# Moving the PSUM evacuation of the attention heads' outputs from VectorE to ScalarE

## The reference

```python
def windowed_gqa_attention(h, w_qkv, w_o, sink):      # h: 1024 tokens x 1024, already normed
    q, k, v = split(h @ w_qkv)                        # 16 query heads, 4 key/value heads, 64 wide
    def block(qi, i):                                 # 128 queries against up to 384 keys
        logits = einsum('bqkgd,bskd->bkgqs', qi, kb) - slopes * dist   # masked outside the window
        m = maximum(max(logits), sink)
        p = exp(logits - m)
        probs = p / (sum(p) + exp(sink - m))
        return einsum('bkgqs,bskd->bqkgd', probs, vb)
    return concat(blocks) @ w_o
```

## Time and profile before

| | |
|---|---|
| median of 3 runs | 2630.5 us |
| profiled execution | 2631.06 us, of which the span is 2629.4 us |
| busy in the span | PE 2330.4 us (89%), DVE 1869.7 us (71%), ACT 1552.1 us (59%), POOL 282.9 us (11%) |
| mean granted TensorE clock | 0.951 |
| first attention | from the start to about 469 us |
| L575, ScalarE's copies of the turned tiles | 88 |
| L657, VectorE's copies of the heads' outputs | 64 |

### The profile page before, as it was taken

How to read it: one execution, slowest core, us unless ns; L and a number is a source line. 1 busy time by engine, 2 the same in 40 slices (tenths; PEclk the granted TensorE clock), 3 DMA queues, 4 the chain that set the end, 5 groups by cost and what they waited for, 6 DMA issues and landing times. The chain is left out here.

```text
span 2629.4 us, 34467 instructions
## 1 busy us (share of the span) xinstructions
PE 2330.4 (89%) x11464; PEld 1758.9 (67%) x11464; DVE 1869.7 (71%) x2461; ACT 1552.1 (59%) x2036; POOL 282.9 (11%) x260
## 2 busy tenths in 40 slices
PE   7899989569999999929999999998955999999991
PEld 6666658447777777727777777776844777777671
DVE  5775572668898888858556666556256888888895
ACT  5554460447777777735555565555043778777772
POOL 0000020012121111030000000002001122211102
PEclk9999999779999999959999999999977999999996
DMA  3012020469999999852000000002146999999995
GB/s 121 25 55 96 24 72 32 170 227 397 392 395 399 402 394 395 338 174 89 24 24 24 24 24 24 0 24 72 32 171 206 390 394 401 398 394 393 403 360 212
DMA packets 129501, 538.48 MB, mean 205 GB/s; under 512 B 23232, under 2 KB 52032, under 8 KB 80288
## 3 DMA queue, kind: packets, MB, share of 16 engines
q1 hardware_dynamic: 110496, 470.62, 47.1%
q0 software_dynamic: 18944, 67.12, 7.3%
HBM read 487.50 MB, written 50.20 MB: 204 GB/s over the span
## 5 line engine op out<-in xcount | busy, mean ns | idle before, releaser
L1507 DVE TENSOR_TENSOR m_lo_gate<-m_raw_gate,m_hi_gate 128x2048 fp32r<-128x2048 f32 x132 | 298.9, 2290 | 81.7 <-ACT m_hi_gate L1502 79.8
L1507 DVE TENSOR_TENSOR m_lo_up<-m_raw_up,m_hi_up 128x2048 fp32r<-128x2048 f32 x128 | 292.5, 2285 | 7.1 <-ACT m_hi_up L1502 7.0
L1507 DVE TENSOR_TENSOR m_lo_down<-m_raw_down,m_hi_down 128x2048 fp32r<-128x2048 f32 x124 | 280.2, 2283 | 13.7 <-ACT m_hi_down L1502 13.7
L1502 ACT CAST m_hi_down<-m_raw_down 128x2048 fp32r<-128x2048 f32 x124 | 236.2, 1907 | 90.7 <-DMA m_raw_down<-in_moe_w_down_dram 54.8
L1502 ACT CAST m_hi_gate<-m_raw_gate 128x2048 fp32r<-128x2048 f32 x132 | 247.8, 1908 | 25.6 <-DMA m_raw_gate<-in_moe_w_gate_dram 25.4
L1502 ACT CAST m_hi_up<-m_raw_up 128x2048 fp32r<-128x2048 f32 x128 | 244.4, 1911 | 22.2 <-DMA m_raw_up<-in_moe_w_up_dram 21.2
L1622 PE MATMUL m_G<-m_hi_gate,m_x_hi 128*96 128x512 f32 x512 | 206.1, 402 | 11.4 <-DVE m_x_lo L1732 11.3
L1622 PE MATMUL m_U<-m_hi_up,m_x_hi 128*96 128x512 f32 x512 | 205.2, 401 | 0.0
L1623 PE MATMUL m_G<-m_hi_gate,m_x_lo 128*96 128x512 f32 x512 | 204.6, 400 | 0.0
L1624 PE MATMUL m_G<-m_lo_gate,m_x_hi 128*96 128x512 f32 x512 | 202.5, 395 | 0.0
L1623 PE MATMUL m_U<-m_hi_up,m_x_lo 128*96 128x512 f32 x512 | 201.8, 394 | 0.0
(11 more groups left out here) (380 smaller groups left out, 4907.9 us busy)
## 6 DMA issues: line engine op xcount, KB each, us to landing
m_raw_gate<-in_moe_w_gate_dram SPq DMA_DIRECT2D x128, 1024.0 KB, 11.1
m_raw_up<-in_moe_w_up_dram SPq DMA_DIRECT2D x128, 1024.0 KB, 12.8
m_raw_down<-in_moe_w_down_dram SPq DMA_DIRECT2D x124, 1024.0 KB, 12.0
out_rows<-m_y POOLq DMA_DIRECT2D x64, 384.0 KB, 7.5
a1n_rows<-in_diff_w_qkv_dram SPq DMA_DIRECT2D x21, 512.0 KB, 5.5
out_rows<-a0n_gain SPq DMA_DIRECT2D x1, 8064.0 KB, 37.3
x_res<-in_x_dram SPq DMA_DIRECT2D x4, 1024.0 KB, 9.6
a0n_rows<-in_swa_w_o_dram SPq DMA_DIRECT2D x8, 512.0 KB, 3.3
```

Source lines behind the costliest of these rows:

```text
L1502: act.copy(self.hi[w][:, cut], self.raw[w][:, cut]).then_inc(self.hi_done[w], 1)
L1507: eng.tensor_tensor(self.lo[w][:, cut], self.raw[w][:, cut], self.hi[w][:, cut].bitcast(F32), ALU.subtract)\
```

## The change

`heads_out` goes from VectorE's program to ScalarE's. The two `tensor_copy` become two `act.copy` of the same operands. On ScalarE they stand behind the copies of block `i` and concern block `i-1`; those of block 7 stand behind the loop. On VectorE the calls are taken out, and nothing is put in their place. Semaphores and counts stay as they are.

```diff
@@ scalar engine, group(g, last_group)
+                    def heads_out(i):
+                        act.wait_ge(pv_done, 8 * g + i + 1)
+                        out = O[:, i % 2, :].rearrange("p (h n) -> p h n", h=QH)
+                        for e, part in enumerate(HALVES):
+                            last = act.copy(oT[part, i, bass.ds(2 * g, 2), :], out[part, e:QH:2, :])
+                        last.then_inc(oT_ready, 1)
@@
                             act.copy(pT[:, i % 2, j, :], TB[:, (before[i] + j) % 2, :]).then_inc(pT_ready, 1)
+                        if i >= 1:
+                            heads_out(i - 1)
                         if i == 3 and not last_group:
                             projections.high_part(act, g + 1, 2)
+                    heads_out(NT - 1)
@@ vector engine, group(g, last_group)
-                    def heads_out(i):
-                        dve.wait_ge(pv_done, 8 * g + i + 1)
-                        out = O[:, i % 2, :].rearrange("p (h n) -> p h n", h=QH)
-                        for e, part in enumerate((slice(0, 64), slice(64, 128))):
-                            last = dve.tensor_copy(oT[part, i, bass.ds(2 * g, 2), :], out[part, e:QH:2, :])
-                        last.then_inc(oT_ready, 1)
@@
                             normalise(i)
-                        if i >= 1:
-                            heads_out(i - 1)
                         if i == 4 and not last_group:
                             projections.low_part(dve, g + 1, 2)
                     if last_group:
                         o_part(0)
                         o_part(1)
-                    heads_out(NT - 1)
```

## The result

The changed kernel takes 2648.7 us in the median of 4 runs (2645.9 to 2650.7) against 2630.3 before: ratio 1.0066, 95% interval 1.0050 to 1.0082, 18.4 us slower. I had predicted 15.3 us slower, 2645.8 us, with a range of 2638 to 2652. The profiled execution took 2648.4 us (span 2646.7).

The account below looks back on a forecast made before the run. TensorE sets the loops' pace, with ScalarE very near and VectorE third. Losses of 9.4 us in three groups, 3.3 in the last and 2.6 at its end sum to 15.3 us slower: 2645.8 us, range 2638 to 2652.

Parts of the forecast that it names:

- Rival D: VectorE as hidden pacemaker: freeing 0.86 us in each of 32 blocks shortens them; 4.4 us faster, 2626.1; chance 2%.
- h = 0.87 us: ScalarE's cost per heads_out: 0.11 us of lost overlap plus two copies of 0.38 us.
- The offset `2 * g`: Dynamic offset on ScalarE, computed while the third copy runs, at nothing; some 0.1 us if not covered.
- 3.14 us a group: Loss in each of groups 0 to 2, summed over the block steps; 9.4 us in three.
- 3.33 in the last group: Last group's steps: 0.87 for block 1 to 2, 2.44 for four steps, 0.02 for block 6 to 7.
- no wait for `a_snk`: Sign in the last group: ScalarE's 0.26 us wait for VectorE's stats disappears, hiding part of the new copies.
- 2.57 at the end: Behind the last group, L587 queues behind heads_out(7), so the output projection starts 2.57 us later.
- rival B: The gap at the last group's end drops TensorE's clock, costing 1.4 to 2 us more; 2647.5 us; chance 25%.
- the prediction's own sign: Listed as proving the prediction wrong: a clock below 1 behind 378 us, which would point to rival B.
- the bare forecast: The forecast alone, h near 0.87 and TensorE's clock kept: 15.3 us slower, 2645.8 us; chance 45%.
- Rival A: The 64-partition copies on ScalarE overlap, so h = 0.55; sum 8.8 us slower, 2639.3 us; chance 15%.
- C: ScalarE's copies cost more than their columns say, near h = 1.29; sum 24.6 us slower, 2655.1 us; chance 10%.

Follow-up runs that it names:

- the gap placement: Changed kernel with heads_out(i-1) on ScalarE moved between its second and third copy of block i; ratio 1.0011, 2.9 us slower than before by the ratio.
- without copies: Changed kernel without the 64 copies, ScalarE only waiting and signalling, so later work computes on other data; ratio 1.0074.
- the parts: Two kernels with heads_out on ScalarE only in groups 0 to 2 (ratio 1.0036), or only in the last group (1.0030), on VectorE otherwise.
- the kernel with matmuls in the gap: Changed kernel with three extra 512-column matmuls on TensorE, useless for the output, behind the last product; ratio 1.0055.
- the last group alone: heads_out on VectorE in groups 0 to 2 and on ScalarE in the last group; ratio 1.0030, 7.3 us slower than before at the medians.
- the full-height kernel: Changed kernel with each two 64x256 copies replaced by two of 128x256, the second to a spare tensor; ratio 1.0035, 9.6 us slower than before.
- upper half: Changed kernel with only the copy of the upper 64 partitions, even heads' outputs not taken out; 2647.7 us, run once.
- lower half: Changed kernel with only the copy of the lower 64 partitions, odd heads' outputs not taken out; 2640.4 us, run once.

## Why the prediction was right, and by how much it was short

- *ScalarE paces the loops, VectorE nothing.* Shown three ways: the gap placement takes the loops' cost away with the work unchanged, without copies VectorE's relief gives 0.0 us in groups 0 to 2, and the parts add up. Rival D (VectorE as pacemaker) is out.
- *h = 0.87 us.* Measured 0.88 to 0.89 (6.27 to 7.16, 4.88 to 5.77). The total is right and its parts are not quite: the copies are 0.367 long, in all 0.77 from start to start, and the missing 0.11 isn't ahead of them but before the next block's first copy. It sits in the upper half's copy, not in 64 partitions as such. So the total came out for a reason that was in part wrong., from which I read that height ends the overlap, fit this too: the second of the two L557 writes the upper half, and the last read of PSUM before that L543 is L553's of the upper half. No run tests these rows. The offset `2 * g` cost nothing, as forecast: its 46 ns (a row of ScalarE's sequencer at L551) leave the 0.48 us from the third copy to L551 as it is between other instructions.
- *3.14 us a group.* Steps give 0.34 + 0.32 + 0.89 + 0.80 + 0.89 + 0.03 = 3.27, so 9.8 instead of 9.4.
- *3.33 in the last group.* 3.39 in the repeated profile, with the four steps from block 1 to 5 at 7.13 to 7.15 and no wait for `a_snk`, as forecast. In the first profile 5.50, 2.1 more through low clock.
- *2.57 at the end.* The wait was 2.45, but the end cost 4.1 in both profiles: the clock falls behind the gap each time. This is the term that was mis-sized: the sum had the clock at nothing. I had it as rival B, at 25%, priced 1.4 to 2; it measured 1.6, in the change and its repeat (4.1 less 2.45) and between them and the kernel with matmuls in the gap (98.6 less 97.0), and 2.8 in the profile of the last group alone. By the prediction's own sign (a clock below 1 behind the last group) the bare forecast was wrong there and B right. It belonged into the sum.

With it the sum is 9.8 + 3.4 + 4.1 = 17.3 us. The two medians, 18.4 and 15.3, lie on both sides of it; a run of this kernel carries some us of chance (before: 2624.6 to 2636.1 in 23 runs). That the repeat's median is the forecast's 15.3 to the tenth is luck. A part of that chance is in the attention, and the forecast had no term for it: the step from block 0 to 1 takes 4.5 us in some groups and about 6 us in others, in the profiles of both kernels. Rival A was wrong in its sum but holds for copies that start at partition 0, as the full-height kernel shows; C didn't come.

What stays open: why a copy from the upper half, over four exponentials, still delays the next copy by 0.11 us, and what decides in which steps, of the last group and at the start of the others, the clock falls.

## What to carry to other kernels

Before moving work to an engine with idle time, find which of its gaps the work will stand in: here 0.75 us cost 0.89 a block behind the copies and nothing 1.8 us earlier, in a wait of the same engine. Look at what is queued behind the moved piece when its loop ends, since there a wait is no longer a block old. Relief for VectorE, which already waited in each block, was worth nothing in groups 0 to 2, though it was busy for 71% of the span.

## What the runs showed of the hardware

- ScalarE copies of 64x256 from PSUM take 0.367 us; with the lower 64 partitions they overlap their neighbours by 0.10 us, with the upper 64 they don't (0.61 instead of 0.48 before, 0.39 instead of 0.27 behind).
- Behind the last group a gap of TensorE of 2.8 us was followed by some us at the 1.2 GHz level in all four profiles that had it (the change, its repeat, the gap placement, the last group alone). So were the gaps of 2.58 (full height), 2.43 (upper half), 2.31 (lower half) and 2.12 us (no copies); the one of 1.11 us wasn't, and with matmuls in the gap the clock stayed.
- In the last group of the change VectorE's `stats` are done just as GpSimd's L423 starts, and it's L660 that takes longer while L423 runs, off the path: four scalings took 3.19 us there instead of 1.41.

```profile
356.78 3.19 DVE L660 TENSOR_SCALAR a_probs<-a_probs,a_inv 128x384 f32<-128x384 f32 x4
```
```profile
356.42 2.35 POOL L423 TENSOR_TENSOR a0n_lo<-a0n_rows,a0n_hi 128x1024 fp32r<-128x1024 f32 x1 [7.57 <-ACT a0n_hi L419]
```
